# Two more slots in the ring of expert weights: in both layers, a half of the row copies' buffer and the routers' scratch

## The reference, cut to what matters

```
# layer 1 (hierarchical_moe)
xs = tok[order // TOP_K]                          # rows sorted by expert
hg = lax.ragged_dot(xs, w_gate, sizes)            # w_gate, w_up: 32 x 1024 x 256
hu = lax.ragged_dot(xs, w_up, sizes)
ys = lax.ragged_dot(jax.nn.silu(hg) * hu, w_down, sizes)   # w_down: 32 x 256 x 1024
out = jnp.einsum('nkd,nk->nd', ys[inv].reshape(N, TOP_K, D), weights)

# layer 2 (moe_ffn), the same with 64 experts, and a shared expert that sees every token
yb = swiglu(h_pad[tok], w_e_gate[e], w_e_up[e], w_e_down[e]) * wt[:, None]
return swiglu(h, w_sh_gate, w_sh_up, w_sh_down) + routed[:n]
```

## Time and profile before

| | us |
|---|---|
| runs | 2088.35, 2083.51, 2076.02 |
| median | 2083.51 |
| the profiled execution, its device time | 2081.98 |
| its span (first to last instruction) | 2079.8 |
| mean granted TensorE clock, share of full speed | 0.963 |
| PE busy | 1882.6 |
| DMA: share of the 16 engines by SP's queue q1 | 55.9% |
| DMA: share by POOL's queue q0 | 11.2% |

### The profile page before, as it was taken

One profiled execution on the slowest core, in us unless ns is written; L12 is line 12 of the kernel. 1 busy time (PEld: TensorE's weight loads), 2 busy tenths in 40 slices (PEclk: granted clock), 3 DMA queues, 4 the chain that ended last, 5 costly groups with the idle time before them and its releaser, 6 DMA issues.

```text
span 2079.8 us, 32419 instructions
## 1 busy us (share of the span) xinstructions
PE 1882.6 (91%) x13222; PEld 1272.2 (61%) x13223; DVE 856.7 (41%) x1997; ACT 553.0 (27%) x1028; POOL 472.8 (23%) x523
## 2 busy tenths in 40 slices
PE   5999999788887899999999999999999899999766
PEld 3777788654444688777666677456556555556332
DVE  3144634443221423523776323254444443343226
ACT  4142612411211432413776203011111121111111
POOL 1000000032221100010543000134454453445310
PEclk9999999889999999799999999999999999999998
DMA  8664631479999532143676143479999998999877
GB/s 339 243 236 172 239 144 62 162 311 417 416 414 404 224 132 81 61 81 101 143 143 128 65 172 122 149 278 405 389 373 370 407 406 344 396 381 404 347 277 298
DMA packets 103192, 532.31 MB, mean 256 GB/s; under 512 B 28082, under 2 KB 28386, under 8 KB 48380
## 3 DMA queue, kind: packets, MB, share of 16 engines
q1 hardware_dynamic: 64208, 457.73, 55.9%
q0 software_dynamic: 36256, 64.54, 11.2%
q10 hardware_dynamic: 2572, 7.81, 1.0%
HBM read 524.34 MB, written 51.90 MB: 277 GB/s over the span
## 4 chain that ended last, share of the span: by engine, by line
PE 73%; DMA 16%; DVE 5%; ACT 3%; issue 2%; SPq 1%; POOL 0%; ACTq 0%; POOLq 0%; DVEq 0%
PE ps L253 31%; PE ps L1763 17%; DMA arena<-in_egu 11%; PE ps L1837 9%; DMA arena<-in_ada 3%; PE ps L1729 3%; PE ps L413 2%; PE ps L3062 1%; PE ps L1824 1%; PE ps L435 1%; PE ps L2292 1%; PE ps L3088 1%; PE ps L1085 1%; DMA arena<-h_rows,arena 1%; DMA arena<-y_rows 1%
## 5 line engine op out<-in xcount | busy, mean ns | idle before, releaser
L1763 PE MATMUL ps<-arena 128*64 128x256 f32 x4096 | 484.5, 391 | 64.6 <-DMA arena<-in_egu 53.1
L1763 PEld LDWEIGHTS ps<-arena 128*64 128x64 f32 x4096 | 298.6, 141 | 270.1 <-issue 80.5
L253 PE MATMUL ps<-arena 128*128 128x256 f32 (+4 forms) x1268 | 321.4, 412 | 13.2 <-issue 5.3
L253 PEld LDWEIGHTS ps<-arena 128*128 128x128 f32 (+1 forms) x1268 | 221.9, 198 | 96.0 <-issue 68.7
L1711 POOL DMA_INDIRECT arena<-h_rows,arena x160 | 190.0, 1188 | 277.4 <-DVE arena L1703 122.7
L1717 POOL DMA_INDIRECT y_rows<-arena x160 | 160.2, 1001 | 396.2 <-DVE arena L1868 333.3
L1837 PE MATMUL ps<-arena 128*64 128x512 f32 x1024 | 242.2, 602 | 7.0 <-DVE arena L1832 3.0
L1832 DVE COPY arena<-ps 128x256 f32<-128x256 f32 (+1 forms) x96 | 36.5, 380 | 420.4 <-PE ps L1824 420.4
L1811 ACT ACTIVATE arena<-ps 128x256 f32<-128x256 f32 (+1 forms) x96 | 33.4, 348 | 510.6 <-PE ps L1763 510.6
L3026 POOL DMA_DIRECT2D arena<-in_nabias x160 | 85.3, 541 | 303.8 <-PE ps L2904 176.1
L1837 PEld LDWEIGHTS ps<-arena 128*64 128x64 f32 x1024 | 66.2, 136 | 101.9 <-issue 96.7
(11 more groups left out here) (433 smaller groups left out, 2734.0 us busy)
## 6 DMA issues: line engine op xcount, KB each, us to landing
arena<-in_egu SPq DMA_DIRECT2D x204, 1024.0 KB, 13.0
arena<-in_ed SPq DMA_DIRECT2D x102, 1024.0 KB, 9.8
arena<-in_ada SPq DMA_DIRECT2D x48, 1024.0 KB, 7.1
arena<-in_win SPq DMA_DIRECT2D x37, 1024.0 KB, 5.1
arena<-y_rows SPq DMA_DIRECT2D x20, 1024.0 KB, 13.9
arena<-in_nabias POOLq DMA_DIRECT2D x96, 128.0 KB, 5.4
arena<-in_wout SPq DMA_DIRECT2D x8, 1024.0 KB, 7.3
h_rows<-arena ACTq DMA_DIRECT2D x8, 512.0 KB, 3.2
```

The source lines that it names most:

```text
L253: z = pe.matmul(o, l, r, start=start and i == 0, stop=stop and i == len(pairs) - 1, skip_group_check=check)
L1763: z = pe.matmul(b[64 * j:64 * j + 64, 256 * s:256 * s + 256], XV[:, c, 64 * h:64 * h + 64], wk(k)[:, j * 256:j * 256 + 256], start=k == 0, ...
```

## The change

Two slots are added to the ring: 15, the second half of the row copies' buffer (`SCR_AT + 2048`), and 16, the region from `LOW + 32` on, which in the expert part held only the routers' scratch (the same memory is slot 11 of the ring, used for other data after layer 1's experts).

```diff
         LATER = [LOW + 32, LOW + 2080, LOW + 4128, LOW + 14336]
-        ring = Ring(book, "ring", slots + [A[:, o:o + 2048] for o in MORE1 + LATER])
+        LAST = SCR_AT + 2048
+        ring = Ring(book, "ring", slots + [A[:, o:o + 2048] for o in MORE1 + LATER + [LAST, LOW + 32]])
...
             for i in (0, 1, 2):
                 sp_more(xa, (NS + i + 2, NS + i), [(n2, ("hrows", 3)), (n2, ("tm", 3, 1)), (xa.st, ("xg", 0))])
+            sp_more(xa, (NS + 2, NS + 10), [(n2, ("w", 3))])
+            sp_more(xa, (NS + 6, NS + 9), [(n2, ("hrows", 3)), (n2, ("tm", 3, 1)), (xa.st, ("xg", 0))])
...
         def sp_xb(sp, w):
-            for i, at_ in enumerate((6, 7, 8)):
+            sp_more(xb, (3, NS + 10), [(sh, ("d", 3, 1)), (xb.st, ("part", 2)), (xb.st, ("xg", 0))])
+            for i, at_ in enumerate((6, 7, 8, NS + 9)):
                 sp_more(xb, (i + 3, at_), [(n3, ("hrows", 3)), (n3, ("tm", 3, 1)), (sh, ("gu", 1, 1)), (xb.st, ("xg", 0))])
```

## The result

The changed kernel takes **2065.95 us** (median of 9 runs) against 2083.51 us, ratio 0.9917, 95% interval 0.9898 to 0.9936: 13 to 21 us less. The forecast was 2067. The profiled execution has a span of 2059.7 us, where before it was 2079.8.

The account below looks back on a forecast made before the run. Layer 1's experts were taken as DMA-bound, layer 2's as alternating between full DMA and full PE. Terms 3.3 - 0.5 - 1.0 + 12.0 + 1.5 = 15.3 us off 2081.98 gave 2067 us, range 2056 to 2080.

Parts of the forecast that it names:

- layer 2's body: Layer 2's experts: a two-load lead fills DMA pauses and removes PE waits and slow clock; 12.0 us gained.
- Layer 1, gross: Layer 1's head: two loads start earlier in idle DMA time, 2.5 us each, less 1.7 given back; 3.3 us gained.
- First gather: Layer 1's head: the load released early runs beside the gather that all wait for; 0.5 us lost.
- Layer 1's tail: End of layer 1: the second projection weight lands one expert later, about where the last gathers run; 1.0 us lost.
- Layer 2's head: Start of layer 2: SP stands at slot 16 and load 7 is delayed, at no cost; lead of two loads stays.
- The 1.5 taken off for uneven pace: Layer 2's experts: 13.5 us cut to 12.0, for uneven load pace and an expert's two gathers falling together.
- Further blocks: After layer 2's experts: first loads start two slots earlier, ahead of a gather taking 7.07 us; 1.5 us gained.
- Only the heads: Rival: only the layers' starts gain, pauses inside layer 2 move but don't shrink; 2075, or 2077 with costs; chance 0.22.
- Gathers behind the loads: Rival, slower: gathers in both layers and the further blocks queue behind SP's loads; 2096 us; chance 0.07.
- All of it: Rival: every layer 2 wait and its slow clock go, layer 1 gains too; 26 us, so 2056; chance 0.11.
- sign of being wrong: Gathers' time to landing grows with the queue; also named: layer 2's experts keep their length, or a new slot 16 wait.

Follow-up runs that it names:

- l2_join_late: Kernel before, with the two slots joining layer 2's ring only at the loads of expert 16: ratio 0.9955 to before.
- l2_leave_early: Layer 1 as before; layer 2 starts with eleven slots, and the two leave its ring at the loads of expert 10: ratio 1.0002 to before.
- the kernel that closes it: Changed kernel with two slots leaving layer 1's ring after expert 7, not 5, and the context loaded after expert 9, not 8: ratio 0.9906 to before.
- l1_only: Kernel before, with the two slots added in layer 1's list alone: ratio 0.9976 to before.
- after_again: The changed kernel once more, unchanged, for a second profile on chip 6: ratio 0.991 to before.
- l2_16_last: Changed kernel with slot 16 last in layer 2's list in place of seventh: ratio 0.9949 to before.
- l2_only: Kernel before, with the two slots added in layer 2's list alone: ratio 0.9946 to before.
- before once more: The kernel before, unchanged, profiled a second time on chip 14: layer 2 596.6 us from first to last gate part, layer 1 270.6 us.
- the floor: PE's own time for layer 2, 570 us; kernel before with half-size expert loads there took 575.0 us, first to last gate part, 4.7 of it ACT waits.

## Why the prediction was right

The number was right, 2067 for 2066, and the mechanism was: a lead of loads is carried into the stretches where DMA is full, the pauses inside layer 2 are filled, and the slow clock behind the waits goes with them. Joining late and leaving early show it for layer 2. That the number came within 1 us is partly luck. The forecast's terms sum to 15.3 us; measured in the first pair of profiles they sum to 3.8 - 0.5 + 17.7 + 1.5 = 22.5. The spans of that pair differ by 20.1, because the changed kernel came 2.84 us late to the experts, the medians by 17.6, and the forecast was taken from an execution 1.5 us below the median. The term that was mis-sized is layer 2's body: 12.0 us, measured 17.7 in the first pair and 7 to 8 on chips 0 and 14.

- **Layer 1, gross: right.** Forecast 3.3 us from 2.5 + 2.5 - 1.7. Measured 3.2 to 3.8 by first gate part to y_rows (267.5, 267.5 and 267.6 in three more profiles, 270.6 and 270.7 before; the other kernels with layer 1 as before have 269.3 to 271.5). The 1.7 given back is the pause of the window above. That it is this pause, the kernel that closes it supports.
- **First gather, 0.5 us: not shown.** From the first expert load to the first gate part the first pair of profiles gives 93.13 and 93.67. But `l1_only`, `after_again` and `l2_16_last`, with the new load beside the gather, have 93.2 to 93.3, while kernels without it reach 96.4. The cost is nothing that can be seen.
- **Layer 1's tail, 1.0 us: wrong.** The gather at the earlier trace rows took 3.69 us and takes 3.81: 0.1 us.
- **Layer 2's head, slot 16's wait at no cost: right**, by `l2_16_last`. That its two loads of lead make no gain at that place, but later, the kernel that leaves early shows.
- **Layer 2's body, 12.0 us: too small for the first pair, 17.7.** Up to the gate part at 1722.85 I had 8.5 us; it now starts at 1711.47, 10.8 us earlier counted from the layer's first gate part. From there on I had 3.6 + 1.4 - 1.5, and measured 6.9. The 1.5 taken off for uneven pace was wrong: no run shows it. And the gate part at 1722.85 itself ran slow (8.51 us against 7.13) and now runs at full clock, 1.4 us that I left out. With both, 3.6 + 1.4 + 1.4 = 6.4 of 6.9. Of the first half, 2.3 us have no term of mine. The wait that the profile puts down to DVE at 1860.40 went with the others, as I held.
- **On other chips the same term is too large.** With PE's waits on the ACT copy there (0 in the first profile, 5.3 and 8.5 us in `l2_only` and `l2_join_late`), first to last gate part falls by 7 to 8 us in place of 12.0 (596.2 to 589.1 on chip 0, 596.6 to 588.6 on chip 14), and layer 2's length by 11, not 18. A likely reason, not tested by itself: with nine slots such a wait falls into time in which PE would wait for loads anyway; with eleven it is on the path.
- **Further blocks, 1.5 us: right in size, the reason not in the first pair but in the others.** Last gate part to the load of y_rows went from 75.6 to 74.1 us. In this pair the gather of the earlier trace rows went from 7.07 to 6.76 only, and 1.3 us came from the first block's gate part (6.40 to 5.13 us for the same work), which takes anything from 5.0 to 6.7 us with nine slots as with eleven. But PE's wait for that gather is 6.8 us in `l1_only`, 6.7 in before once more and 6.4 in `l2_leave_early`, which end the layer with nine slots, and 3.3 to 6.4 in `l2_only`, `l2_join_late` and the three on chip 6 with eleven. With eight and seven slots it is 8.0 and 8.1. So more slots do shorten this wait, by 0.3 to 3.5 us in the pairs on one chip and in the first pair, and on chips 0 and 14 this is most of why the length falls by more than the body.
- **Rivals.** Only the heads: fell with the two kernels on chip 14. Gathers behind the loads: fell with the landing times (7.5 to 7.4 us in layer 1, 8.6 to 8.8 in layer 2, loads 18.4 to 21.2), so two loads more in SP's queue cost a gather at most 0.2 us. By the Trainium skill, "DMA: Bandwidth & Descriptors", section "Queues, rings and completion order", a DMA engine takes turns between the queues that have work, and the trace agrees. All of it: two waits on egu are left, and 10 us above the floor. The prediction's sign of being wrong, a growth of the gathers' time with the queue, did not show.

## What to carry to other kernels

When a kernel changes between stretches where DMA is full and stretches where the engine is, a buffer more is worth something only if a pause of DMA comes ahead of a full stretch that it can fill: look for DMA shares below 1 ahead of a plateau, not at the plateau's height. It need not be there from the start, and it must not leave before the plateau. Expect less from each further buffer, and much more loss from one taken away (here some 20 us for the ninth; 7 for the tenth and 4 for the eleventh on one chip, 18 for both in the first pair); add to the waits that go the slow clock behind them, read from the rows, and work out the floor from waits and clock before asking for more buffers.

## What the runs showed of the hardware

- **The clock ahead of the change moves the time by nearly as much as the change.** From 150 to 330 us, ahead of all experts, all kernels run the same work. Windows (columns as in the earlier trace rows) of before, before once more, and after once more:
```profile
150.00:330.00 180.00, 171.54 (x1432) 143.52 (x1432) 93.75 (x184) 61.85 (x92) 0.00 (x0) 0.98 0.46 170
```
```profile
150.00:330.00 180.00, 171.68 (x1399) 145.19 (x1400) 90.00 (x171) 61.02 (x91) 0.00 (x0) 0.95 0.46 170
```
```profile
150.00:330.00 180.00, 171.60 (x1352) 143.57 (x1349) 86.33 (x159) 59.10 (x87) 0.00 (x0) 0.91 0.45 170
```
  At a granted clock of 0.98 the first expert load starts at 329.6 us, at 0.95 at 334.6, at 0.91 at 341.4. What lowered it I did not find. Runs of the kernel before on chip 6 spread over 15 us, and the long ones have the lower mean clock (2075.4 us at 0.963, 2090.8 at 0.957). At equal mean clock over the whole execution (0.966) the runs on chip 6 have spans of 2073.5 to 2073.9 before and 2056.6 to 2057.7 after: 16 to 17 us, without the spread.
- **A release from PE that comes 1.0 us late on two of the chips.** At one place in layer 2, before (first profile), and before once more on chip 14:
```profile
1410.49 0.44 PE L1824 MATMUL ps<-arena 128*128 128x128 f32 x2
1410.61 0.38 ACT L1811 ACTIVATE arena<-ps 128x256 f32<-128x256 f32 x1 [6.22 <-PE ps L1763]
```
```profile
1417.62 0.44 PE L1824 MATMUL ps<-arena 128*128 128x128 f32 x2
1417.90 1.04 PE L1729 MATMUL ps<-arena 128*128 128x128 f32 x8
1418.74 0.38 ACT L1811 ACTIVATE arena<-ps 128x256 f32<-128x256 f32 x1 [6.62 <-PE ps L1729]
1419.61 1.94 PE L1837 MATMUL ps<-arena 128*64 128x512 f32 x8 [0.49 <-ACT arena L1737]
```
  In the first, ACT copies 0.12 us after the two transposes start. In the second only when the next eight matmuls are nearly through, 1.12 us after. PE then waits for what ACT does next. Of the 14 profiles, seven on chips 0 and 14 have 4 to 10 such waits in layer 2 (2.2 to 8.5 us). The seven-slot kernel on chip 0 has none, but it has the late copies. What ended ACT's idle time before line 1811 (1812 in the changed file), before and then with seven slots, 1340 to 1940 us:
```profile
ACT arena L1811 <- PE ps L1763: 302.2, 63, 12.6
```
```profile
ACT arena L1812 <- PE ps L1764: 225.2, 39, 12.8
ACT arena L1812 <- PE ps L1825: 105.2, 17, 6.7
```
  In the first two profiles and the four on chip 6 every such release is put down to the gate matmuls. In all eight on chips 0 and 14, 15 to 17 of them are put down to the two transposes behind the gate part. With seven slots PE waits for loads so often that the late copies cost it nothing. So the late copies go with the chip. The cause is open.
